# A two-block transformer kernel: another placement of its buffers in SBUF

## The reference

```python
def first_block(x, ...):                      # two layers of this
    z = rms_norm(x, norm_mix_w) @ w_in + b_in            # 1024 x 5640
    ya = dilated_mixture_attention(rope(aq), rope(ak), av)   # 8 heads of 64
    hm = mlstm_chunkwise(silu(conv(mq)), silu(conv(mk)), mv, mi, mf)  # 4 heads of 128
    mixed = sigmoid(ga) * (ya @ w_proj_att) + sigmoid(gb) * (yb @ w_proj_mlstm)
    x = x + mixed @ w_out
    x = x + square(relu(rms_norm(x, norm_mlp_w) @ w_ff1)) @ w_ff2      # 1024 x 4096 x 1024

def second_block(x, ...):                     # one layer
    proj = _rmsnorm(h, norm1_w) @ w_in
    # a state-space scan (16 heads of 64), attention to the 128 best-scored keys,
    # and a windowed pooling branch, each gated and projected up to 1024
    merged = g0 * (y_ssd @ w_up_ssd) + g1 * (y_att @ w_up_attn) + g2 * (y_pool @ w_up_pool)
    h = h + merged @ w_out
    a, b = split(_rmsnorm(h, norm2_w) @ w_ffn_in)
    return h + (silu(a) * b) @ w_ffn_out       # 1024 x 5632, 2816 x 1024
```

## Time and profile before

| | us |
|---|---|
| median of the three timed runs | 2529.86 |
| the profiled execution: its time | 2530.58 |
| the profiled execution: its span, first to last instruction | 2528.8 |
| PE busy in the span | 2458.0 |
| POOL busy | 1098.9 |
| DVE busy | 991.2 |
| ACT busy | 870.1 |

### The profile page before, as it was taken

One profiled execution on the slowest core, in us unless ns is written; L12 is line 12 of the kernel. 1 busy time (PEld: TensorE's weight loads), 2 busy tenths in 40 slices (PEclk: granted clock), 3 DMA queues, 4 the chain that ended last, 5 costly groups with the idle time before them and its releaser, 6 DMA issues.

```text
span 2528.8 us, 30042 instructions
## 1 busy us (share of the span) xinstructions
PE 2458.0 (97%) x11732; PEld 1994.5 (79%) x11732; DVE 991.2 (39%) x1582; ACT 870.1 (34%) x1093; POOL 1098.9 (43%) x808
## 2 busy tenths in 40 slices
PE   8899999999999999899999999999999999999998
PEld 6767788888888867688888888798776688888887
DVE  4545564310212354564320212557585534322202
ACT  4255333331323345333431323442234323322213
POOL 4332345554544422335554554342343245555543
PEclk9999999999999999999999999999999999999999
DMA  4221223223322221223222322231122133223221
GB/s 138 84 67 51 67 84 100 86 98 100 100 100 88 84 67 51 79 71 100 83 100 100 100 99 69 84 92 51 52 88 67 55 100 100 89 93 100 100 100 67
DMA packets 174028, 215.18 MB, mean 85 GB/s; under 512 B 7652, under 2 KB 155044, under 8 KB 173924
## 3 DMA queue, kind: packets, MB, share of 16 engines
q1 hardware_dynamic: 171572, 210.39, 25.9%
q10 hardware_dynamic: 2352, 3.31, 0.4%
HBM read 211.20 MB, written 2.10 MB: 84 GB/s over the span
## 4 chain that ended last, share of the span: by engine, by line
issue 49%; POOL 30%; PE 19%; DMA 0%; POOLq 0%; DVE 0%; ACT 0%; SPq 0%
POOL w_lo L290 30%; PE ps L331 3%; PE ps L330 3%; PE ps L329 3%; PE ps L736 3%; PE ps L1755 2%; PE ps L1753 2%; PE ps L1757 2%; DMA w_raw<-in_w_in 0%; POOLq L301 0%; PE ps L322 0%; PE ps L355 0%; PE ps L349 0%; PE ps L348 0%; PE ps L319 0%
## 5 line engine op out<-in xcount | busy, mean ns | idle before, releaser
L290 POOL TENSOR_TENSOR w_lo<-w_raw,w_hi 128x512 fp32r<-128x512 f32 x804 | 1098.7, 1399 | 1403.2 <-ACT w_hi L276 1391.2
L276 ACT ACTIVATE w_hi<-w_raw 128x2048 fp32r<-128x2048 f32 x200 | 382.9, 1915 | 1033.0 <-PE ps L331 394.0
L736 PE MATMUL ps<-h_hi,w_hi 128*128 128x512 f32 (+1 forms) x936 | 393.8, 421 | 15.1 <-POOL w_lo L290 12.9
L736 PE MATMUL ps<-h_hi,w_lo 128*128 128x512 f32 (+1 forms) x936 | 369.0, 394 | 0.0
L736 PE MATMUL ps<-h_lo,w_hi 128*128 128x512 f32 (+1 forms) x936 | 368.5, 394 | 0.0
L329 PE MATMUL ps<-h_hi,w_hi 128*128 128x512 f32 x816 | 319.0, 391 | 0.0
L331 PE MATMUL ps<-h_hi,w_lo 128*128 128x512 f32 x816 | 317.5, 389 | 0.0
L330 PE MATMUL ps<-h_lo,w_hi 128*128 128x512 f32 x816 | 317.4, 389 | 0.0
L736 PEld LDWEIGHTS ps<-h_hi,w_hi 128*128 128x128 f32 (+1 forms) x936 | 175.8, 188 | 76.2 <-issue 23.1
L736 PEld LDWEIGHTS ps<-h_lo,w_hi 128*128 128x128 f32 (+1 forms) x936 | 175.6, 188 | 43.1 <-issue 7.5
L736 PEld LDWEIGHTS ps<-h_hi,w_lo 128*128 128x128 f32 (+1 forms) x936 | 175.2, 187 | 41.4
(11 more groups left out here) (408 smaller groups left out, 3665.6 us busy)
## 6 DMA issues: line engine op xcount, KB each, us to landing
w_raw<-in_w_in SPq DMA_DIRECT2D x72, 1024.0 KB, 5.2
w_raw<-in_w_ff SPq DMA_DIRECT2D x64, 1024.0 KB, 5.2
w_raw<-in_w_ffn_in SPq DMA_DIRECT2D x22, 1024.0 KB, 5.1
w_raw<-in_w_out SPq DMA_DIRECT2D x12, 1024.0 KB, 5.1
w_raw<-in_w_ffn_out SPq DMA_DIRECT2D x11, 1024.0 KB, 4.9
w_raw<-in_w_proj_att SPq DMA_DIRECT2D x4, 1024.0 KB, 5.0
w_raw<-in_w_proj_mlstm SPq DMA_DIRECT2D x4, 1024.0 KB, 5.1
w_raw<-in_w_up_ssd SPq DMA_DIRECT2D x4, 1024.0 KB, 5.3
```

The lines of the kernel that those rows point to most:

```text
L276: act.activation(k.whi[:, slot * SLOT:(slot + 1) * SLOT], k.wraw[:, slot * SLOT:(slot + 1) * SLOT], ACT.Copy).then_inc(k.hi_done, CHUNKS)
L290: pool.tensor_tensor(k.wlo[:, a:a + T], k.wraw[:, a:a + T], k.whi[:, a:a + T], ALU.subtract)\
L736: mm = pe.matmul(out, lhs, rhs, start=i == 0 and n == 0, stop=stop and n == 2)
```

## The change

`keep` is called in another order and the arena goes behind the kept tensors. `ARENA`, the fixed size of the arena, is gone; its size for the assertion is now whatever SBUF has left.

```diff
-ARENA = 25728
@@ program
         k = Kern(nc, ctx)
+        k.xT = k.keep("xT", KD * T)
         k.hhi, k.hlo = k.keep("h_hi", KD * T, F32R), k.keep("h_lo", KD * T, F32R)
-        k.arena, k.arena_words = (k.top + 127) // 128 * 128, ARENA
-        k.top = k.arena + 4 * ARENA
+        k.wraw = k.keep("w_raw", 2 * SLOT)
         k.whi, k.wlo = k.keep("w_hi", 2 * SLOT, F32R), k.keep("w_lo", 2 * SLOT, F32R)
-        k.xT = k.keep("xT", KD * T)
-        k.wraw = k.keep("w_raw", 2 * SLOT)
         k.cst = k.keep("constants", C_END)
@@
         k.rtok = k.root[:, TT:2 * TT]
+        k.arena = (k.top + 127) // 128 * 128
+        k.arena_words = (nc.sbuf_usable_end() - k.arena) // 4 if callable(nc.sbuf_usable_end) else (nc.sbuf_usable_end - k.arena) // 4
```

## The result

The changed kernel takes 2550.68 us (four runs, 2549.31 to 2552.08) against 2529.95 for the kernel before (four runs, 2529.71 to 2530.58): a ratio of 1.0082, 95% interval 1.0064 to 1.0099, 20.7 us slower. The forecast was 2529.9 with a range of 2526 to 2534. It was wrong.

The account below looks back on a forecast made before the run. PE's matmul pace was taken to bound the kernel; every term was 0, so the sum stayed 2530.58 - 1.78 = 2528.8 us span, forecast as the median 2529.9 us, range 2528 to 2532, and 2526 to 2534 for 8 in 10.

Parts of the forecast that it names:

- What bounds the kernel: Whole kernel: PE is busy 2458.0 of 2528.8 us, so the time is PE's pace plus 70.8 us idle.
- the lever: Distance between matmul starts in the weight stream: one nanosecond over 9648 matmuls is worth 9.6 us.
- Matmuls: Term for PE's matmuls: their time does not depend on operand addresses; value 0, bounds -124 and +58 us.
- The natural experiment: Trace of before: weights fixed, moving operands h_hi, ff_hi and ys_lo at different distances, all 389 ns; taken as no address effect.
- a second witness: Full-precision lines L1220 and L1208, operands in one tensor or in two: 592 and 591 to 592 ns, read as no effect.
- an upper bound of 6 ns a matmul: Matmul term: distance could rise from 226 to 232 ns, seen beside a first-layer stage; +58 us on the whole stream.
- the 9648 and the 6336: Matmul counts: 9648 of 512 columns or their like in the weight stream; 6336 with h_hi or h_lo and weights.
- The slower rival: Matmuls with h and weights: starts a multiple of 16,384 apart hinder each other, +38 us, 2568 us; chance 0.10.
- The two rules weighed: Skill's 216 ns for 512 columns (about 2431 us if reached) against TensorE never waiting for others (sum zero); trace favoured the second.
- The way of the weights: Weight chain through DMA, ACT and POOL: 3.35 us slack a unit, so address effects there cost nothing; value 0.
- DVE and ACT: Stages beside the weight stream: DVE instructions take the same time wherever operands lie; value 0, bound 1 us either way.
- start and end: First weight transfer (10.20 us), setup_x and stored output: value 0, bound 0.1 us for both together.

Follow-up runs that it names:

- run h: Model left out: 55 groups of 24 matmuls on alternating tile pairs, small offsets, other column counts, other types; 215.8 ns in bfloat16, 429.2 in full float32, whatever the difference.
- run d: Model left out: 85 groups of 24 fp32r matmuls, tile starts moved by 0 to 1024 bytes; 226.65 ns at difference 0, 233.3 at 128.
- run a: The changed kernel with its arena 128 bytes higher; 2530.27 us, ratio 1.0001 to the kernel before.
- g: The kernel before with w_hi and w_lo 128 bytes higher and what lies behind them 256; 2574.99 us, ratio 1.0182.

## Why the prediction was wrong

*What bounds the kernel.* Right, and the lever too: PE's distance is the time, and the loss is up to 6.65 ns on each of a count of matmuls.

*Matmuls: the step that failed.* "So neither distance nor a neighbour in the same 16 KB shows. I take 0 for this term." The natural experiment was none in the respect that counts. `h_hi` starts at 16,512, `ff_hi` at 49,280, `ys_lo` at 131,456 and `w_hi` at 152,192; each leaves the remainder 128 modulo 256. The three moving operands differed in region and in distance, never in remainder against the weights, so 389 ns in three groups could say nothing on it. What stood in place of the 0 is 6.65 ns for each matmul whose moving operand came to lie 128 bytes off the weights modulo 256, 21.1 us over the arena's 3408. The rows on L1220 and L1208, offered as a second witness, are of full-precision matmuls, which run h shows to be indifferent in any case. The same section then named the very case without data, "nor one that is 128 bytes off a multiple of 512, which it makes of the arena", and beside it an upper bound of 6 ns a matmul. On the arena's 3408 matmuls that bound is 20 us, and it was left out of the range.

That the bound came so near was luck. It was read from four distances of 232 ns in the earlier trace rows, taken as the pace beside a stage. They come right behind two matmuls of another stage (L1220), and the pace beside a stage is not 232: all such distances of L736 with `h`, the long breaks left out, have a mean of 228.3 ns. In run d too a group starts with distances of up to 236 ns even at equal remainders and settles at 227. The counts are near but not exact: the trace of before has 8952 matmuls of 512 columns with weights (5544 with `h`, 3408 with the arena) and 1248 narrower ones with the weights moving, for the 9648 and the 6336 of the text.

*The slower rival* had the right kind of mechanism, remainders of the two operands, and by the same luck nearly the right price, but the wrong tensors and the wrong sign. It looked for the loss in L329 to L331 and not in L1753 to L1757, and it came there and in the other matmuls with the arena, not in those with `h`. It held that equal remainders hinder. Equal remainders modulo 256 are the good case, and `h` and `w_hi` kept theirs. The argument against it, that the weight blocks pass through many remainders, was hollow: they pass in steps of 512 bytes, all of one remainder modulo 256.

*The two rules weighed.* The rule of the Trainium skill ("SBUF — State Buffer", section "SBUF: two separate sides") that TensorE waits for no other engine is not contradicted: in run d no other engine works during the groups and the effect is there. It was taken to exclude an effect of placement, which it does not say; the effect hangs on TensorE's own two operands. And the 216 ns of the Trainium skill ("TensorE: Matmul & The Clock Gate", section "Back-to-back issue gap"), which the page gives for a matmul by itself, agrees with the stream in bfloat16, 215.8 ns in run h. The 10.8 ns above it came with the type fp32r, and none of the placements tried takes them away.

*The way of the weights, DVE and ACT, start and end.* Right. Run a has all of these moves and none of the loss; POOL went from 1399 to 1395 ns, ACT stayed at 1915, DVE went from 688 to 689, and PE's idle time changed by 1.3 us.

*The numbers.* The chance of slower was 0.10. The rows supported no more than this: three kinds of tensors of one remainder tell nothing about another. With that said, "no effect" and "6 ns on what changes its remainder" should have stood side by side, and the range should have reached 2550.

## What to carry to other kernels

With fp32r operands, matmuls of 512 columns and a fresh weight load for each, keep the start of the moving tile and that of the weights equal modulo 256 bytes: 226.7 ns against 233.3. In this kernel a move costs nothing as long as the distance to the weights stays a multiple of 256 (run a), and the rounding `(top + 127) // 128 * 128` does not see to that. For other column counts the best difference is another, and has to be measured. When several rows are called as witnesses that an address does not matter, first write down their remainders: if these are all alike, there is one witness.

## What was not expected of the hardware

- In fp32r the time of a matmul depends on the address of one operand against that of the other, down to a single element of 4 bytes: at 512 columns 226.65 ns at equal remainders, 228.75 at 64, up to 236.45 at 4 bytes. In bfloat16 and full float32 it does not, at differences of 32 to 192.
- At a difference of 128 the distances follow a steady rhythm with no other engine at work: 229 and 238 ns in turn, or seven distances from 228 to 241 ns. Both occur for the same remainders (runs d and g). One rhythm or the other makes 0.9 ns a matmul.
- After a change of tiles the first distances are often longer, up to 236 ns at equal remainders in run d, before the steady 226.7.
- The sign of the effect depends on the columns: at 256 equal remainders are the slow case (120.0 against 117.4 to 118.75 ns) and at 448 too (206.3 against 200.35 at 64), at 480 and 512 the fast one.
